# A third kind of token block, another order of experts, three output buffers and earlier loads in a mixture-of-experts kernel

## The reference

```python
scores = sigmoid(h @ w_router)                 # best group of 4 experts by scores + bias, then its top 2
gates  = sum(one_hot(top_e) * top_w, axis=-2)  # two experts per token, weights normalised
a, g   = h @ w1[e], h @ w3[e]                  # 1024 -> 256, for every expert e
out    = sum_e (silu(a) * g * gates[e]) @ w2[e]  # 256 -> 1024
```

## Time and profile before

| | us |
|---|---|
| median of 3 runs | 1092.4 (1092.16 to 1094.26) |
| profiled execution, own time | 1093.52 |
| its span in the profile | 1091.7 |
| MoE of layer 0, first up to end of last down | 353.17 to 546.7 |
| MoE of layer 1, first up to end of last down | 892.59 to 1048.2 |
| TensorE busy in the whole span | 809.1 (74%) |

### The profile page before, as it was taken

How to read it: one execution, slowest core, us unless ns; L and a number is a source line. 1 busy time by engine, 2 the same in 40 slices (tenths; PEclk the granted TensorE clock), 3 DMA queues, 4 the chain that set the end, 5 groups by cost and what they waited for, 6 DMA issues and landing times.

```text
span 1091.7 us, 13835 instructions
## 1 busy us (share of the span) xinstructions
PE 809.1 (74%) x4044; PEld 517.1 (47%) x4044; DVE 345.8 (32%) x756; ACT 211.5 (19%) x513; POOL 122.2 (11%) x181
## 2 busy tenths in 40 slices
PE   4799997789961898776608999987898438986720
PEld 2675554447850343334307655544577414443400
DVE  0102103752755212111145021046527632221127
ACT  1310003441010121121114100044510001221110
POOL 0210100100111010001134000000002110011021
PEclk9899998999965898888858999989999559999875
DMA  9952493782435976976366332328410377569341
GB/s 381 363 198 93 167 413 107 310 345 80 141 148 198 388 256 224 376 288 224 107 228 276 119 113 77 104 80 322 181 77 20 125 284 285 193 226 351 122 136 64
DMA packets 39836, 223.58 MB, mean 205 GB/s; under 512 B 5008, under 2 KB 5840, under 8 KB 22832
## 3 DMA queue, kind: packets, MB, share of 16 engines
q1 hardware_dynamic: 19008, 155.50, 37.1%
q0 software_dynamic: 12240, 50.22, 13.1%
q10 hardware_dynamic: 8480, 16.33, 4.2%
HBM read 194.70 MB, written 27.33 MB: 203 GB/s over the span
## 4 chain that ended last, share of the span: by engine, by line
PE 57%; DVE 12%; issue 9%; DMA 8%; ACT 5%; PEld 5%; PEldq 2%; ACTq 1%; POOL 1%; POOLq 0%; DVEq 0%; SPq 0%
PE psum L498 17%; PE psum L628 7%; PE psum L637 6%; PE psum L495 6%; PE psum L583 4%; PE psum L669 3%; PEld psum L583 3%; DMA moe_rows<-shared 3%; DMA big<-in_weights 3%; PE psum L658 3%; PE psum L615 3%; ACT shared L1001 2%; PE psum L447 2%; PE psum L603 2%; DMA shared<-moe_rows,ridx 1%
## 5 line engine op out<-in xcount | busy, mean ns | idle before, releaser
L498 PE MATMUL psum<-big 128*128 128x384 f32 x576 | 190.9, 488 | 2.7 <-issue 2.7
L498 PEld LDWEIGHTS psum<-big 128*128 128x128 f32 x576 | 108.8, 190 | 78.4 <-issue 8.3
L637 PE MATMUL psum<-big,shared 128*64 128x256 f32 x576 | 84.8, 455 | 47.1 <-issue 34.9
L1485 DVE TENSOR_SCALAR shared<-shared 128x128 f32<-128x128 f32 (+1 forms) x28 | 7.0, 251 | 283.4 <-ACT shared L1010 283.4
L628 PE MATMUL psum<-big,shared 128*128 128x512 f32 x160 | 81.6, 669 | 9.9 <-ACT shared L1001 6.8
L637 PEld LDWEIGHTS psum<-big,shared 128*64 128x64 f32 x576 | 52.9, 164 | 75.1 <-issue 44.2
L583 PE MATMUL psum<-big 128*128 128x256 f32 x384 | 83.9, 380 | 2.0 <-ACT big L947 1.8
L583 PEld LDWEIGHTS psum<-big 128*128 128x128 f32 x384 | 72.7, 190 | 12.9 <-issue 3.2
L495 PE MATMUL psum<-big 128*128 128x256 f32 x288 | 69.4, 402 | 8.4 <-DMA big<-in_weights 4.7
L447 PE MATMUL psum<-const,big 128*128 128x128 f32 x160 | 31.4, 309 | 51.3 <-ACT big L838 27.8
L495 PEld LDWEIGHTS psum<-big 128*128 128x128 f32 x288 | 57.6, 203 | 18.9 <-issue 7.1
(11 more groups left out here) (217 smaller groups left out, 912.7 us busy)
## 6 DMA issues: line engine op xcount, KB each, us to landing
big<-in_weights SPq DMA_DIRECT2D x80, 1024.0 KB, 6.9
big<-in_experts SPq DMA_DIRECT2D x22, 2048.0 KB, 11.4
big<-in_experts SPq DMA_DIRECT2D x22, 1024.0 KB, 6.9
moe_rows<-ln_b POOLq DMA_DIRECT2D x3, 3584.0 KB, 25.5
moe_rows<-shared ACTq DMA_DIRECT2D x20, 256.0 KB, 5.2
moe_rows<-shared ACTq DMA_DIRECT2D x36, 128.0 KB, 3.8
ln_b<-in_ln POOLq DMA_DIRECT2D x4, 1024.0 KB, 6.2
gate_b<-mod_rows POOLq DMA_DIRECT2D x4, 1024.0 KB, 7.0
```

The costliest lines, as they stand in the source:

```text
L498: ins = pe.matmul(bank(name)[:, 0:T], w[piece][:, k, part * P:(part + 1) * P], hT[:, k, :], start=(k == 0), stop=(k == KC - 1))
L637: ins = pe.matmul(psD[HALF * j:HALF * j + HALF, 0:DE], xT[:, k * P:k * P + HALF], w[:, 2 * DE * k + DE * j:2 * DE * k + DE * j + DE], star ...
```

## The change

The change has these parts.

- A third kind of block, for up to 32 tokens. Its up is eight times four calls, four 32-column strips with 128 output columns each (`up_quarter_block`); its hidden transpose is two matmuls with pieces of the identity; its down is two times four calls with 256 output columns each. TensorE, ScalarE and VectorE choose among three kinds (0 full, 1 half, 2 quarter) with nested branches. The columns of w1 and w3 are packed on the host in four pieces of 64 instead of two of 128.
- The experts are ranked from both ends of the size order in turn: largest, smallest, second largest, second smallest, and so on. For this the number of active experts is computed ahead of the ranking.
- There are three output buffers `yo`, each with its own semaphore. A quarter block is stored with four transfers instead of two.
- SyncE issues the up and the down weights of ranks 0 and 1 together as soon as the ranking is known. The wait for the first transposes is gone.
- `tokens_T` of the next block is moved ahead of the down matmuls, in the stage and in its loops.

With the same tokens, layer 0 has 5 full, 2 half and 8 quarter blocks after the change (5 full and 10 half before), and layer 1 has 5 full, 1 half and 7 quarter (5 full and 8 half before).

```diff
-                load_up(L, 0)
-                load_up(L, 1)
+                for r in range(2):
+                    load_up(L, r)
+                    load_down(L, r)
                 sp.wait_ge(table_ready, L + 1)
...
-                first = sp.value_load(tabu[0:1, T_FIRST:T_FIRST + 1], min_val=1, max_val=BLOCKS * DEPTH + 1)
-                sp.wait_ge(xT_full, first + L + 2)
-                stop_here(sp, "sp")
-                load_down(L, 0)
-                load_down(L, 1)
                 for r in range(2, E):
...
+            def up_quarter_block(L, i, w):
+                pe.wait_ge(xT_ready, i + L + 1)
+                pe.wait_ge(hid_ready, i)
+                for k in range(KC):
+                    for j in range(4):
+                        ins = pe.matmul(psD[QUART * j:QUART * j + QUART, 0:P], xT[:, k * P:k * P + QUART],
+                                        w[:, 2 * DE * k + P * j:2 * DE * k + P * j + P],
+                                        start=(k == 0), stop=(k == KC - 1), skip_group_check=True)
+                ins.then_inc(up_full, 1)
...
+            def hidden_T_quarter(i):
+                pe.wait_ge(hid_ready, i + 1)
+                strips = ident.rearrange("p (k w t) -> p w k t", k=2, w=2)
+                for n in range(2):
+                    ins = pe.matmul(psB[HALF * n:HALF * n + HALF, 0:HALF].rearrange("p (k t) -> p k t", k=2),
+                                    hid[:, 0:HALF], strips[:, n, :, :], start=True, stop=True, skip_group_check=True)
+                ins.then_inc(hidT_full, 1)
...
+            def down_quarter_block(after, w):
+
+                pe.wait_ge(hidT_ready, after)
+                pe.wait_ge(yo_ready, after)
+                for k in range(2):
+                    for n in range(4):
+                        ins = pe.matmul(psC[QUART * n:QUART * n + QUART, 0:256], hidT[:, QUART * k:QUART * k + QUART],
+                                        w[:, UP + D * k + 256 * n:UP + D * k + 256 * n + 256],
+                                        start=(k == 0), stop=(k == 1), skip_group_check=True)
+                ins.then_inc(down_full, 1)
...
                 with pe.If(full_blocks > 0):
                     up_full_block(L, start, w)
                 with pe.Else():
-                    with pe.If(end > 0):
-                        up_half_block(L, start, w)
+                    with pe.If(end > 2):
+                        up_quarter_block(L, start, w)
+                    with pe.Else():
+                        with pe.If(end > 0):
+                            up_kind(L, start, w)
+                        stop_here(pe, "pe")
+                    stop_here(pe, "pe")
+                with pe.If(end > 0):
+                    tokens_T(L, start + 1)
                     stop_here(pe, "pe")
                 following = expert_table(r + 1) if r < E - 1 else None
                 if r:
                     last_down(L, r - 1, end_before, start)
                 with pe.If(end > 0):
-                    tokens_T(L, start + 1)
...
                     with pe.If(full_blocks > 1):
                         with pe.Fori(1, full_blocks) as j:
                             up_full_block(L, start + j, w)
+                            tokens_T(L, start + j + 1)
                             down_full_block(start + j, w)
-                            tokens_T(L, start + j + 1)
                             hidden_T_full(start + j)
...
                         with pe.If(end > 1):
-                            up_half_block(L, start + full_blocks, w)
+                            with pe.If(end > 2):
+                                up_quarter_block(L, start + full_blocks, w)
+                            with pe.Else():
+                                up_kind(L, start + full_blocks, w)
+                            tokens_T(L, start + full_blocks + 1)
                             down_full_block(start + full_blocks, w)
-                            tokens_T(L, start + full_blocks + 1)
-                            hidden_T_half(start + full_blocks)
+                            with pe.If(end > 2):
+                                hidden_T_quarter(start + full_blocks)
+                            with pe.Else():
+                                hidden_T_half(start + full_blocks)
...
+                        def through(b):
+                            act.wait_ge(down_full, after)
+                            act.wait_ge(yo_out[b], after // 3 * 64 + 64)
+                            act.activation(yo[b][:, 0:n], psC[:, 0:n], copy).then_inc(yo_ready, 1)
+                            act.wait_ge(yo_ready, after + 1)
+                            for c in range(D // width):
+                                at = c * width if strips == 1 else 0
+                                top = 0 if strips == 1 else rows * c
+                                act.dma_start(moe_d[bass.ds(j * P, rows), width * c:width * c + width],
+                                              yo[b][top:top + rows, at:at + width]).then_inc(yo_out[b], 16)
+                            if strips < 4:
+                                act.sem_inc(yo_out[b], 32)
...
+                link(ts(grid(1, 1, E), quarts.rearrange("p (u e) -> p u e", u=1), 0.0, None, ALU.is_gt))
+                link(dve.tensor_reduce(tab[:, T_ACTIVE:T_ACTIVE + 1], pair[:, 1, 0:E], AX.X, ALU.add))
+                link(ts(st[:, 6:7], tab[:, T_ACTIVE:T_ACTIVE + 1], 2.0, -1.0, ALU.mult, ALU.add))
+                link(stt(key, num[:, 0:E], -1.0 / (2 * E), quarts, ALU.mult, ALU.add))
                 link(tt(grid(0, E, E), rows(key, E), cols(key, E), ALU.is_gt))
                 link(dve.tensor_reduce(rank, grid(0, E, E), AX.X, ALU.add))
+                link(ts(key, rank, -2.0, st[:, 6:7], ALU.mult, ALU.add))
+                link(stt(rank, rank, 2.0, key, ALU.mult, ALU.min))
```

More of the change, by code:

```diff
@@ L42 @@
 HALF = 64
+QUART = 32
 BLOCKS = (2 * T - E) // P + E
@@ L709, in stage @@
                     with pe.Else():
-                        hidden_T_half(start)
-                    with pe.If(full_blocks + end > 2):
-                        pe.wait_ge(down_in[r % BUFS], (L * (E // BUFS) + r // BUFS + 1) * 16)
+                        with pe.If(end > 2):
+                            hidden_T_quarter(start)
+                        with pe.Else():
+                            hidden_T_half(start)
+                        stop_here(pe, "pe")
+                    with pe.If(full_blocks > 0):
+                        with pe.If(full_blocks + end > 2):
+                            pe.wait_ge(down_in[r % BUFS], (L * (E // BUFS) + r // BUFS + 1) * 16)
+                            stop_here(pe, "pe")
                         stop_here(pe, "pe")
@@ L1021, in copied @@
                         act.activation(hidT[:, 0:n], psB[:, 0:n], copy).then_inc(hidT_ready, 1)
-                    with act.If(half_block > 0):
-                        copied(P)
-                    with act.Else():
-                        copied(DE)
-                def block_out(after, j, half_block):
-                    def stored(n, pieces):
-                        act.wait_ge(down_full, after)
-                        act.wait_ge(yo_stored, after * 32)
-                        act.activation(yo[:, 0:n], psC[:, 0:n], copy).then_inc(yo_ready, 1)
-                        act.wait_ge(yo_ready, after + 1)
-                        for rows, columns, piece in pieces:
-                            act.dma_start(moe_d[bass.ds(j * P, rows), columns:columns + 512], piece).then_inc(yo_stored, 16)
-                    with act.If(half_block > 0):
-                        stored(512, [(HALF, 512 * n, yo[HALF * n:HALF * n + HALF, 0:512]) for n in range(2)])
-                    with act.Else():
-                        stored(D, [(P, 512 * n, yo[:, 512 * n:512 * n + 512]) for n in range(2)])
+                    by_kind(kind, lambda: copied(DE), lambda: copied(P), lambda: copied(HALF))
@@ new lines, in block_out, with stored @@
+                def block_out(after, j, kind):
+                    def stored(n, strips):
+                        rows, width = P // strips, min(n, 512)
+                        def through(b):
[10 more added lines that the diff above has]
+                                act.sem_inc(yo_out[b], 32)
+                        with act.If(after % 3 > 1):
+                            through(2)
+                        with act.Else():
+                            with act.If(after % 3 > 0):
+                                through(1)
+                            with act.Else():
+                                through(0)
+                            stop_here(act, "act")
+                    by_kind(kind, lambda: stored(D, 1), lambda: stored(512, 2), lambda: stored(256, 4))
+                    stop_here(act, "act")
@@ L1623, in _ @@
                 pool.wait_ge(xT_ready, first + count + L + 1)
-                pool.wait_ge(yo_stored, (first + count) * 32 + 32)
```

(5 more changed lines are left out.)

137 lines of the change are left out of this document (78 added, 59 removed).

## The result

The changed kernel takes 1183.85 us (median of 4 runs, 1180.56 to 1187.46) against 1092.28 before: a ratio of 1.084, 95% interval 1.080 to 1.088. It is slower, as forecast, but by 92 us instead of 25. The profiled execution has a span of 1182.4 us.

What follows compares the result with a forecast made beforehand. The prediction took TensorE, waiting for its own code, to bound the kernel. Layer 0 at -3 and layer 1 at +27 gave +24 or +25 on 1092.4, so 1117; eight-in-ten range 1080 to 1145, bounds of the parts 1102 to 1135.

Steps and rivals of the forecast that it cites:

- The walk over empty stages: Layer 1's seven stages without tokens, at the end: from 5.98 to 10 us each, less 7.3 slack, +21.
- the late first gather: Start of each layer's MoE: more VectorE operations, first gather among early weight loads; +7 a layer, bounds 0 to 9.
- Small stages with quarters: Small experts' stages, shorter work but 10 us of code: 11.5 us each, bounds 7.0 to 15; before 12.3 and 10.9.
- -7 and +4: Change over nine small stages in layer 0 and seven in layer 1, at 11.5 us each.
- rival 3: Stalls multiply: each quarter stage stalls twice and takes 15 us; total 1173, likelier 1145; chance 0.13.
- Alternating sizes: Order of experts: a large expert's loop doesn't fetch the code of the quarter after it; counted 0.
- Row transposes before the down: Full blocks: token copy lies beside the down, about 1 us for each of 10; -5 a layer (0 to -6).

Runs made afterwards that it cites:

- the full padding: Kernel before, with the quarter's up (twice) and down behind a never-taken branch in every stage, 288 more instructions each: 1179.0 against 1094.4, ratio 1.080.
- the one loop with quarters: The one loop with the quarter kind put back, one copy of its up, down and hidden transpose in a stage: 1088.6, ratio 0.996.
- the one loop: Changed kernel without quarters and with late weights, its stage one loop over an expert's blocks, empty stages left out: 1049.9, ratio 0.961.

## Why the prediction was right in direction and wrong in size

The cause was named: TensorE waits for its own code, and the code of a stage grows. Code that is never executed costs 87 us by itself. That this is close to the whole loss is chance: by the runs above the quarter's code costs 128 us in the changed kernel and the early weights 15, while the strips and the early transposes give back 25 each. The walk over empty stages (+21; 22 measured by leaving it out) and the late first gather (+14; 15) were forecast rightly. The order, counted at nothing, is that. The third buffer was not run alone; with it, the order and the transposes together the kernel is no faster than with the transposes alone.

The step that failed is *Small stages with quarters*: "I take 11.5", and with it -7 and +4. Where such stages stand in a row they took 14.9 us in layer 0 and 14.8 in layer 1, near the bound of 15 and the figure of rival 3, to which I gave 0.13. That rival's picture, two stalls in a stage and slower matmuls, is also what the two stages of the timeline above show. If all sixteen small stages are like these eight, they make 54 of the 62 us by which the active stretches missed: together they grew by 49 instead of shrinking by 13.

Two things were wrong in that step. The first is the rule: I set 10 us of code beside the work of a stage and let the larger count, with a little on top. In the full padding the work of a stage is as before, and its code is longer by 288 / 276 = 1.04 packets of 3.5 us. The small stages in its trace, first up and last down of layer 0 and of layer 1:

```profile
442.40 5.84 PE L637 MATMUL psum<-big,shared 128*64 128x256 f32 x32 [9.50 <-issue]
...
581.37 3.68 PE L690 MATMUL psum<-big,shared 128*64 128x512 f32 x8 [7.48 <-issue]
...
1006.45 3.67 PE L637 MATMUL psum<-big,shared 128*64 128x256 f32 x32 [1.00 <-ACT shared L1033]
...
1110.32 3.68 PE L690 MATMUL psum<-big,shared 128*64 128x512 f32 x8 [7.19 <-issue]
```

They take 15.4 and 14.8 us each instead of 12.3 and 10.9, 3.5 us more on the mean of the sixteen. So the added packet, though only jumped over, is paid nearly whole and not hidden behind the work. The six stages of large experts ahead of them grew by 1.3 us each.

The second is the work. I counted 2.2 us for a quarter's up and 0.9 for its down. On the page of the changed kernel the ups of its 15 quarters take 51.4 us, 3.4 each, and the downs 19.9, 1.3 each: 25 us more in all, which is a part of those 54. The same 64 matmuls at two places of layer 1, each with its stretch (us, then busy us of PE, PEld, DVE, ACT and POOL, the granted clock, DMA share, GB/s):

```profile
972.87 0.38 PE L653 MATMUL psum<-const,shared 128*128 128x128 f32 x2
979.70 3.40 PE L645 MATMUL psum<-big,shared 128*32 128x128 f32 x64 [6.45 <-issue]
979.70:983.10 3.40, 3.40 (x65) 3.20 (x65) 0.00 (x0) 0.00 (x0) 0.00 (x0) 0.56 0.05 16
...
1016.77 1.95 PE L645 MATMUL psum<-big,shared 128*32 128x128 f32 x64
1016.77:1018.72 1.95, 1.95 (x65) 1.68 (x64) 0.00 (x0) 1.02 (x1) 0.00 (x0) 1.00 0.58 223
```

After 6.45 us of standing still they run at a mean granted clock of 0.56, near the lower of TensorE's two levels (1.2 GHz); behind a full block without a gap they run at 1.00 (2.4 GHz). The first place is the quarter of the second expert, behind the first expert's loop of 25 us. That this loop does not bring its code is as *Alternating sizes* had it.

The other term off its size has the opposite sign. *Row transposes before the down* was -10, for 10 full blocks; it is -25. The waits were there: in the two active stretches of the kernel before, TensorE waits 19.0 us for the copy L1001, 12.2 of them ahead of half blocks (layer 0, then layer 1; last, idle time and what ended it):

```profile
L637 PE MATMUL psum<-big,shared 128*64 128x256 f32 x320 | 49.5, 471 | 28.8 <-issue 23.4 <-ACT shared L1001 5.4
L628 PE MATMUL psum<-big,shared 128*128 128x512 f32 x80 | 41.7, 681 | 5.4 <-ACT shared L1001 3.0 <-issue 2.4
...
L628 PE MATMUL psum<-big,shared 128*128 128x512 f32 x80 | 39.9, 657 | 4.5 <-ACT shared L1001 3.8 <-issue 0.7
L637 PE MATMUL psum<-big,shared 128*64 128x256 f32 x256 | 35.4, 434 | 18.4 <-issue 11.5 <-ACT shared L1001 6.8
```

With the transposes alone moved 2.2 us of this are left. I had left the half blocks' share inside the 11.5.

The range was also added up wrongly. The bounds that the prediction names for its parts (starts 0 to 9, transposes -6 to 0, small stages 7.0 to 15, walks 0 to 24 and 0 to 3) make 1005 to 1190, not 1102 to 1135; the measured 1184 lies inside them.

What stays open is how code and work add up in a stage. Estimates from TensorE's busy time a stage and packets of 3.5 us, laid end to end in layer 1: 7.6 and 5.6, so 13.2 us, in the small stages before; 7.4 and 10, so 17.4, in the last four of the changed kernel; 5.9 and 5.7, so 11.6, in the last four of the one loop with quarters. They took 10.9, 14.8 and 11.6. So at most 2.6 us of a stage were hidden, and in one kernel nothing. Nor is the cost proportional to the packets: on the kernel before 18 more cost 28 us and 38 cost 87, from the one loop 18 more cost 39, and in the changed kernel the quarter's 40 cost 128. The clock is a part of it. The mean granted clock of 353 to 547, a share of full speed, is 0.87 before and 0.78 in the changed kernel. The first fence is the kernel before, the second the changed one (columns as above):

```profile
353.00:547.00 194.00, 147.93 (x660) 79.10 (x660) 32.00 (x60) 34.63 (x61) 20.55 (x36) 0.87 0.71 263
```

```profile
353.00:547.00 194.00, 123.30 (x836) 70.39 (x840) 25.10 (x52) 30.18 (x52) 20.75 (x37) 0.78 0.66 244
```

How the loss divides between the waits, the clock and the positions of the branches was not measured by itself.

## What to carry to other kernels

Where one engine runs long unrolled code with branches, count the instructions that it jumps over as well as those it executes: in the full padding 288 of them along the path cost about 3.5 us in a small or an empty stage and 1.3 in the stages of large experts, while the same code out of the path cost nothing. Before adding a special case to an unrolled stage, put the code of that case into the kernel behind a branch that is never taken and time it. Early issue of a large load is not free: it delayed the small transfer that the first step waits for, here by 7 us in each layer.

## What the runs showed of the hardware

- Code that is never executed made the kernel 8% slower in the stages (1.080) and 0.1% behind them (1.001, within its interval).
- The 64 strip matmuls of a quarter's up take 1.95 us when nothing interrupts them, 30 ns each (1016.77 above), half of the 57 ns of strips with twice the columns; the granted clock is 1.00 in both stretches.
- A gather of 128 rows took 4.3 us when no weight load was in flight, and 11.9 and 11.2 us when the loads of three to four experts (3 MB each) had been issued before or beside it.
